# Q, K and index queries projected directly in transposed form, in an fp32 decoder layer on one core

## The reference

```
h    = rmsnorm(x) * norm_g                       # 256 x 2048
proj = h @ w_in                                  # 2048 x 18512, split into sections
(a_u, a_v, a_z, b_bg, b_cg, b_x, b_z, q, k, v, c_z, i_q, i_k, i_w, g_a, g_b, g_c) = proj
y_a  = a_u * (tril(ws) @ a_v + a_b) * silu(a_z)              # per chunk of 128 tokens
y_b  = b_bg * causal_conv3(b_cg * b_x) * silu(b_z)
score[t, s] = sum over 16 heads of i_w[t, h] * relu(i_q[t, h] . i_k[s])      # 64 per head
keys = top 64 of the causal scores of each query
y_c  = softmax(q . k * 128**-0.5 + rel_bias, over those keys) @ v * silu(c_z)  # 8 heads of 128
m    = sigmoid(g_a) * (y_a @ p_a) + sigmoid(g_b) * (y_b @ p_b) + sigmoid(g_c) * (y_c @ p_c)
out  = rmsnorm(x + m @ w_o) * final_g
```

## Time and profile before

| | us |
|---|---|
| median of three runs (lowest to highest) | 1084.79 (1084.78 to 1084.98) |
| span of the profiled execution, first to last instruction | 1083.3 |
| around the span (median less span) | 1.5 |
| TensorE busy | 1065.8 |
| VectorE busy | 602.3 |
| ScalarE busy | 508.4 |

### The profile page before, as it was taken

How to read it: one execution, slowest core, us unless ns; L and a number is a source line. 1 busy time by engine, 2 the same in 40 slices (tenths; PEclk the granted TensorE clock), 3 DMA queues, 4 the chain that set the end, 5 groups by cost and what they waited for, 6 DMA issues and landing times.

```text
span 1083.3 us, 14804 instructions
## 1 busy us (share of the span) xinstructions
PE 1065.8 (98%) x4864; PEld 877.8 (81%) x4864; DVE 602.3 (56%) x719; ACT 508.4 (47%) x627; POOL 33.3 (3%) x41
## 2 busy tenths in 40 slices
PE   6999999999999999999999999999999999999996
PEld 5888788878888888888888888888888888888885
DVE  6544455544566544655555565555555566666455
ACT  7444444444454444654554454444445544444443
POOL 1000000000001300000000000000000000000004
PEclk9999999999999999999999999999999999999999
DMA  7766566666566666556556556666665555566553
GB/s 230 251 193 194 158 190 177 186 180 183 175 192 189 196 193 193 178 177 182 171 171 179 174 180 184 184 186 182 187 183 178 189 189 184 185 223 229 194 194 136
DMA packets 104841, 203.08 MB, mean 187 GB/s; under 512 B 8356, under 2 KB 8520, under 8 KB 104432
## 3 DMA queue, kind: packets, MB, share of 16 engines
q1 hardware_dynamic: 104032, 200.96, 60.8%
q0 software_dynamic: 608, 1.74, 0.5%
q10 hardware_dynamic: 176, 0.07, 0.0%
HBM read 200.63 MB, written 2.11 MB: 187 GB/s over the span
## 4 chain that ended last, share of the span: by engine, by line
PE 97%; DVE 1%; DMA 1%; ACT 0%; issue 0%; SPq 0%; ACTq 0%; DVEq 0%
PE psum L845 31%; PE psum L847 31%; PE psum L846 31%; PE psum L854 2%; DMA keep<-x 1%; DVE hl L610 0%; PE psum L948 0%; PE psum L925 0%; PE psum L974 0%; PE psum L908 0%; PE psum L924 0%; PE psum L960 0%; PE psum L959 0%; PE psum L947 0%; PE psum L958 0%; DVE keep L829 0%
## 5 line engine op out<-in xcount | busy, mean ns | idle before, releaser
L553 DVE TENSOR_TENSOR wl<-raw,wh 128x1024 fp32r<-128x1024 f32 (+1 forms) x370 | 454.3, 1229 | 437.8 <-ACT wh L339 437.7
L339 ACT CAST wh<-raw 128x1024 fp32r<-128x1024 f32 (+1 forms) x370 | 388.4, 1051 | 535.0 <-PE psum L847 532.7
L845 PE MATMUL psum<-wh,hh 128*128 128x512 f32 x1280 | 507.5, 396 | 0.0
L847 PE MATMUL psum<-wh,hl 128*128 128x512 f32 x1280 | 499.2, 390 | 0.0
L846 PE MATMUL psum<-wl,hh 128*128 128x512 f32 x1280 | 498.5, 389 | 0.0
L845 PEld LDWEIGHTS psum<-wh,hh 128*128 128x128 f32 x1280 | 240.4, 188 | 51.1 <-issue 2.9
L847 PEld LDWEIGHTS psum<-wh,hl 128*128 128x128 f32 x1280 | 240.2, 188 | 51.0
L846 PEld LDWEIGHTS psum<-wl,hh 128*128 128x128 f32 x1280 | 240.5, 188 | 48.8 <-issue 0.2
L845 PE MATMUL psum<-wh,yh 128*128 128x512 f32 x192 | 75.0, 391 | 0.0
L847 PE MATMUL psum<-wh,yl 128*128 128x512 f32 x192 | 74.7, 389 | 0.0
L846 PE MATMUL psum<-wl,yh 128*128 128x512 f32 x192 | 74.7, 389 | 0.0
(11 more groups left out here) (134 smaller groups left out, 355.6 us busy)
## 6 DMA issues: line engine op xcount, KB each, us to landing
raw<-w_in SPq DMA_DIRECT2D x288, 512.0 KB, 3.6
raw<-w_o SPq DMA_DIRECT2D x32, 512.0 KB, 3.6
raw<-p_c SPq DMA_DIRECT2D x16, 512.0 KB, 3.5
raw<-p_a SPq DMA_DIRECT2D x16, 512.0 KB, 4.1
raw<-p_b SPq DMA_DIRECT2D x16, 512.0 KB, 3.7
keep<-x SPq DMA_DIRECT2D x4, 512.0 KB, 6.0
keep<-x SPq DMA_DIRECT2D x1, 2048.0 KB, 9.5
keep<-bias_table POOLq DMA_DIRECT2D x1, 1024.0 KB, 8.1
```

Source lines behind the costliest of these rows:

```text
L339: act.copy(wh[:, slot, 0:width], raw[:, slot, 0:width]).then_inc(high_split, 1)
L553: dve.tensor_tensor(wl[:, slot, 0:width], raw[:, slot, 0:width], wh[:, slot, 0:width].bitcast(F32), ALU.subtract).then_inc(low_split, 1)
L845: pe.matmul(dst[t], h, w_h[:, j], start=start, stop=False)
L847: mm = pe.matmul(dst[t], l, w_h[:, j], start=False, stop=stop)
```

## The change

Six chunks, the two of index queries in phase 1 and the four of Q and K in phase 2, are computed by a new function, `product_t`. It makes a block of 128 weight columns stationary and moves the 256 tokens: four column blocks x two row blocks x three = 24 matmuls a sub. The four blocks accumulate in the first halves of banks 0, 1 (blocks 0, 1, copied out by ScalarE) and 6, 7 (blocks 2, 3, copied out by VectorE). The outputs have the columns on the partitions and lie in `keep` and `early` as they are wanted. The 48 transposes, the copies into `iq_s` and `qk_s` and those out of PSUM are gone; one copy of 256 columns per head is left (`iq_t`, `q_t`), and K is read in place.

```diff
+        acc_t = [psum[:, 6 * t:6 * t + 2, 0:SEQ] for t in range(T)]
...
+        def columns(buf, slot, row, i):
+
+            return buf[:, row, bass.ds(slot * N + i * SEQ, SEQ)]
...
         @block_.scalar
...
+            def move_t(q, dst):
+
+                act.wait_ge(tile0_done, q)
+                act.copy(dst.rearrange("p (b t) -> p b t", b=2), acc_t[0]).then_inc(evac[0], 1)
...
+            act.wait_ge(evac[1], CH2)
+            act.wait_ge(evac[0], CH2)
+            def index(first, c, row, dst, evict):
+
                 for g in range(SUB):
                     if g == 0:
-                        act.copy(iq_s, block(keep, IQ, c)).then_inc(iq_ready, 1)
-                    if g == 2:
-                        act.wait_ge(iqt_done, c + 1)
-                        act.copy(iq_t, bank[0][:, 0:SEQ]).then_inc(iqt_ready, 1)
+                        act.copy(iq_t, columns(keep, IQ, row, first - 4 * row + c)).then_inc(iqt_ready, 1)
...
             with act.Fori(0, 8) as c:
                 for g in range(SUB):
                     if g == 0:
-                        for w, slot in enumerate((Q, K)):
-                            act.copy(qk_s[:, w], block(early, slot, c)).then_inc(qk_ready, 1)
-                    if g == 2:
-                        act.wait_ge(qkt_done, c + 1)
-                        act.copy(qk_t, bank[0]).then_inc(qkt_ready, 1)
+                        act.copy(q_t, columns(early, Q, 0, c)).then_inc(qt_ready, 1)
...
         @block_.vector
...
+            def move_t(last, dst):
+
+                dve.wait_ge(sub_used, last + 1)
+                dve.tensor_copy(dst.rearrange("p (b t) -> p b t", b=2), acc_t[1]).then_inc(evac[1], 1)
...
         @block_.tensor
...
+            def product_t(n, slot, g, last, k0, q, after=False):
+
+                pe.wait_ge(low_split, n + 1)
+                w_h, w_l = (w[:, slot].rearrange("p (k c) -> p k c", k=KS) for w in (wh, wl))
+                for b in range(N // P):
+                    half, dst = b // 2, acc_t[b // 2][:, b % 2]
+                    col = slice(b * P, (b + 1) * P)
+                    if g == 0 and b % 2 == 0:
+                        pe.wait_ge(evac[half], q)
+                    if g == 0 and b == 1 and after:
+                        pe.wait_ge(evac[1], q)
+                    for j in range(KS):
+                        h, l = hh[:, k0 + j], hl[:, k0 + j]
+                        stop = last and j == KS - 1
+                        pe.matmul(dst, w_h[:, j, col], h, start=g == 0 and j == 0, stop=False)
+                        pe.matmul(dst, w_h[:, j, col], l, start=False, stop=False)
+                        mm = pe.matmul(dst, w_l[:, j, col], h, start=False, stop=stop)
+                    if last and b == 1:
+                        mm.then_inc(tile0_done, 1)
+                mm.then_inc(sub_used, 1)
...
-            with pe.Fori(0, 4) as c:
+            with pe.Fori(0, 2) as c:
                 for g in range(SUB):
                     product(SUB1 + SUB * c + g, (SUB1 + g) % RING, g, g == SUB - 1, hh, hl, KS * g, CH1 + c, free=evac)
+            for c in range(2):
+                for g in range(SUB):
+                    product_t(SUB1 + 2 * SUB + SUB * c + g, (SUB1 + g) % RING, g, g == SUB - 1, KS * g, CH1 + 2 + c,
+                              after=c == 0)
...
+            with pe.Fori(0, 4) as c:
+                for g in range(SUB):
+                    product_t(SUB2 + SUB * c + g, (SUB1 + g) % RING, g, g == SUB - 1, KS * g, CH2 + c)
+                    if g == 3:
+                        index(c)
+            with pe.Fori(4, 8) as c:
+                for g in range(SUB):
+                    product(SUB2 + SUB * c + g, (SUB1 + g) % RING, g, g == SUB - 1, hh, hl, KS * g, CH2 + c, free=evac)
+                    if g == 3:
+                        index(c)
...
-                    if g == 1:
-                        pe.wait_ge(qk_ready, 2 * c + 2)
-                        for w in range(2):
-                            for t in range(T):
-                                mm = transpose(bank[0][:, (2 * w + t) * P:(2 * w + t + 1) * P], qk_s[:, w, t])
-                        mm.then_inc(qkt_done, 1)
                     if g == 2:
-                        pe.wait_ge(qkt_ready, c + 1)
-                        pe.matmul(bank[1][:, 0:P], qk_t[:, 0:P], qk_t[:, SEQ:SEQ + P], start=True, stop=True)
-                        pe.matmul(bank[1][:, P:384], qk_t[:, P:SEQ], qk_t[:, SEQ:], start=True,
+                        pe.wait_ge(qt_ready, c + 1)
+                        pe.matmul(bank[1][:, 0:P], q_t[:, 0:P], early[:, 1, bass.ds(Q * N + c * SEQ, P)], start=True, stop=True)
+                        pe.matmul(bank[1][:, P:384], q_t[:, P:SEQ], columns(early, Q, 1, c), start=True,
                                   stop=True).then_inc(logit_done, 1)
```

More of the change, by code:

```diff
@@ L175, in trunk @@
         top8 = stats[:, 0:16].rearrange("p (b c) -> p b c", b=2)
[L177 to L178 removed]
+        q_t = keep[:, 1, 13 * N:13 * N + SEQ]
         logit = keep[:, 1, 14 * N:14 * N + 384]
@@ L400, in _ @@
             act.copy(iw[:], bank[5][:, 0:T * IDX_HEADS].rearrange("p (t h) -> p t h", t=T)).then_inc(iw_ready, 1)
-            with act.Fori(0, 4) as c:
+            with act.Fori(0, 2) as c:
                 for g in range(SUB):
@@ L406, in _ @@
                     split_ahead(SUB1, c, SUB, g)
+            for c in range(2):
+                for g in range(SUB):
+                    if g == SUB - 1:
+                        move_t(CH1 + 2 + c, chunk(keep, IQ, c))
+                    split_ahead(SUB1 + 2 * SUB, c, SUB, g)
             act.wait_ge(bias_done, 1)
@@ L410, in _ @@
                 act.copy(keep[:, 0, (8 + i) * N:(9 + i) * N], bank[i]).then_inc(bias_ready, 1)
-            with act.Fori(0, 8) as c:
+            act.wait_ge(evac[1], CH2)
+            act.wait_ge(evac[0], CH2)
+            def index(first, c, row, dst, evict):
                 for g in range(SUB):
                     if g == 0:
-                        act.copy(iq_s, block(keep, IQ, c)).then_inc(iq_ready, 1)
-                    if g == 2:
-                        act.wait_ge(iqt_done, c + 1)
-                        act.copy(iq_t, bank[0][:, 0:SEQ]).then_inc(iqt_ready, 1)
+                        act.copy(iq_t, columns(keep, IQ, row, first - 4 * row + c)).then_inc(iqt_ready, 1)
                     if g == 4:
-                        act.wait_ge(index_done, c + 1)
+                        act.wait_ge(index_done, first + c + 1)
                         for h in range(2):
@@ L423, in _ @@
                     if g == SUB - 1:
-                        move(CH2 + c, chunk(early, c, 0))
-                    split_ahead(SUB2, c, SUB, g)
+                        evict(CH2 + first + c, dst)
+                    split_ahead(SUB2 + SUB * first, c, SUB, g)
+            with act.Fori(0, 2) as c:
+                index(0, c, 0, chunk(early, 2 * c, 0), move_t)
+            with act.Fori(0, 2) as c:
+                index(2, c, 0, chunk(early, 2 * c, 1), move_t)
+            with act.Fori(0, 4) as c:
+                index(4, c, 1, chunk(early, 4 + c, 0), move)
             for c in range(2):
@@ L619, in _ @@
             dve.memset(score, 0.0).then_inc(score_step, 1)
-            with dve.Fori(0, 4) as c:
+            with dve.Fori(0, 2) as c:
                 for g in range(SUB):
@@ L625, in _, with index @@
                     split_ahead(SUB1, c, SUB, g)
-            with dve.Fori(0, 8) as c:
+            for c in range(2):
+                for g in range(SUB):
+                    if g == SUB - 1:
+                        move_t(SUB1 + SUB * (2 + c) + g, chunk(keep, IQ + 1, c))
+                    split_ahead(SUB1 + 2 * SUB, c, SUB, g)
+            def index(first, c, dst, evict):
                 for g in range(SUB):
@@ L630, in _ @@
                         for h in range(2):
-                            dve.wait_ge(relu_ready, 2 * c + h + 1)
+                            dve.wait_ge(relu_ready, 2 * first + 2 * c + h + 1)
                             for t, s in enumerate((slice(0, P), slice(P, 384))):
                                 if t == 0:
-                                    dve.wait_ge(score_step, 4 * c + 2 * h + 1)
-                                dve.scalar_tensor_tensor(score[:, s], relu[:, h, s], iw[:, t, bass.ds(2 * c + h, 1)],
+                                    dve.wait_ge(score_step, 4 * first + 4 * c + 2 * h + 1)
+                                dve.scalar_tensor_tensor(score[:, s], relu[:, h, s], iw[:, t, bass.ds(2 * first + 2 * c + h, 1)],
                                                          score[:, s], ALU.mult, ALU.add).then_inc(score_step, 1)
                     if g == SUB - 1:
-                        move(0, SUB2 + SUB * c + g, chunk(early, c, 1))
-                    split_ahead(SUB2, c, SUB, g)
+                        evict(SUB2 + SUB * first + SUB * c + g, dst)
+                    split_ahead(SUB2 + SUB * first, c, SUB, g)
+            with dve.Fori(0, 2) as c:
```

(29 more changed lines are left out.)

7 lines of the change are left out of this document (2 added, 5 removed).

## The result

| | before | after |
|---|---|---|
| median of the runs in one comparison, us | 1085.09 (19 runs) | 1086.99 (19 runs) |
| ratio, 95% interval | | 1.0017 (1.001 to 1.0023) |
| span of the profiled execution, us | 1083.3 | 1085.0 |

The changed kernel is slower, by 1.9 us. That is inside the 0.2% I called no change, but the interval excludes 1, and the time is 2.4 us over the forecast of 1084.6, at the upper end of its own range (1087.0).

What follows compares the result with a forecast made beforehand. TensorE's instruction stream was taken as the bound (98% busy): products +5.3, transposes -6.0, new wait +0.5, sum -0.2 us on a 1083.3 us span; with 1.5 us around it, 1084.6 us, no change, range 1080.5 to 1092.0.

Steps and rivals of the forecast that it cites:

- s: Start-to-start spacing of the 1152 new 256-column matmuls; taken as 118 ns, with 1.15 us for each nanosecond.
- (a): Reading of the 256-column spacing: the extra time belongs to the moving side, so 116.1 ns, +3.1 us.
- (b): Reading of the 256-column spacing: the extra belongs to the weight load beside it, 13.4 ns per 128 columns; 120.1 ns, +7.8 us.
- the products: Six weight chunks: 576 matmuls of 512 columns (130.6 us) become 1152 of 256 (135.9 us), +5.3 us.
- Rival 1: Slower: loads disturb the matmul stream, 120.0 ns or more; 1087.1 us at 120.1 ns; chance 0.31 together with rival 3 (late evacuation copies).
- the relative of the earlier trace: Index-key projection at the start: same number types, 256 moving but only 80 weight columns, spacing 116.1 ns.
- The transposes: Removed from TensorE: 8 pairs at 0.25 us by the index queries, 8 groups of four at 0.50 in attention; -6.0 us.
- the new wait: First transposed chunk: its second block waits for VectorE's copy out of bank 1, once, +0.5 us.
- The costs taken as nothing: ScalarE's copies and waits, VectorE's evacuations at later chunks and split, weight DMA, and TensorE's queue: claimed to add no time.
- The rule that two read ports keep loads off the stream: Skill's claim that loading the next weights takes no bandwidth from the streaming matmul; the whole change would end at -2.4 us.

Runs made afterwards that it cites:

- the grid: No layer, TensorE alone, 25 streams of 36 fp32r matmuls with 128 to 32 load and 512 to 128 moving columns: 128 x 256 took 118.3 ns, 80 x 256 116.6.
- the whole half alone: The kernel before with its 48 transposes left out and its products unchanged: 1078.79 us, ratio 0.9939.

## Why the prediction was wrong

- **The bound and the method** held. TensorE's stream decided all, and the terms add up: +7.7 - 6.0 + 0.5 = +2.2 us against +1.9 measured.
- **The step that failed** is "I take s = 118 ns, between (a) and (b)". It was 120.0, the number of (b), so the products cost +7.7 us in place of +5.3. Rival 1 with its 120.1 ns and 1087.1 us was the outcome, to 0.1 us; that the time agrees so closely is partly luck, since the kernel before measured 0.3 us longer in this comparison, and the change is +1.9 against rival 1's +2.3. The total crosses zero at (130.6 + 6.0 - 0.5) / 1152 = 118.1 ns, just where I had put s: halfway between +3.1 and +7.8 us for the products lies no case of its own, and neither mechanism gave 118.
- **(b)'s reason** stands only in part, so its number was better than its mechanism. That the load has a part in it is shown by narrowing it, in the kernel (-5.0 us) and alone (120.0 to 113.4, about half of the 13.3 on top). That its tax is proportional to its columns is refuted: 32 columns take nothing off at 512 moving, and 96 gave more than 112 at 256. I had fitted one line through two points that differed in both widths. Where the other half comes from, and how load and stream disturb each other, stays open.
- **(a)** took the relative of the earlier trace rows at its word. It had 80-column loads: those gave 116.6 in the grid too, while with 128 columns no stream of 256 moving columns alone was under 118.3.
- **The transposes** (6.0; with the whole half alone 6.4 in the time, 6.1 in the profile) were right, and so was the length of **the new wait** (0.5; 0.46 in the trace), though its worth in the time isn't shown. The costs taken as nothing were nothing: TensorE waits for no copy of ScalarE, and at no later chunk.
- The rule that two read ports keep loads off the stream ("TensorE: Matmul & The Clock Gate", part 2, step 1, the Trainium skill) would, as the prediction used it, have given -2.4 us. Here the measurement decides against that use, for 256 moving fp32r columns: the only thing changed from 120.0 to 113.4 was the load's width, so a load isn't free beside the stream. Whether it is read bandwidth that the two share no run shows.

## What to carry to other kernels

Making the narrow operand move doubled the matmuls and the loads here, and in a stream with full loads each matmul took some 13 ns more than its columns, at 256 as at 512: count matmuls, not columns alone, and read the surplus from a stream with the same two widths, or measure it. Where two readings of the rows lie on both sides of the point at which the total changes its sign, forecast one of the two mechanisms, not the middle. If transposing operands on the fly is to be saved, first widen what moves past one load (`hh` and `hl` side by side): that turned +1.9 us into -2.2.

## What the runs showed of the hardware

- fp32r with 128-column loads at the upper clock (granted clock 1.00 in these stretches): spacing 119.8, 146.6, 173.2 and 227.7 ns for 256, 320, 384 and 512 moving columns, that is close to columns / 2.4 GHz + 13.3 ns; full loads beside 128 moving columns follow each other every 111 ns.
- With 256 moving columns, streams with 128-column loads stood at 118.3 to 120.0 ns, those with 112 columns at 113.3 or 117.7, with 96 at 116.0 or 118.3, with 64 at 113.4 or 116.6.
- A steady stream has more than one spacing. The same loop held 113.3 and 117.7 ns in different stretches of one execution, going over where a wait or other matmuls interrupt it; 128 x 256 held 118.3 in one stream and 120.0 in others. After a group of transposes the long matmuls took some ten of them, 224 to 236 ns apart, to settle back to 227; that adds some 0.05 us, so that a group costs 0.50 us and not 4 x 0.11. Why is open.
